# Where the mean is subtracted in three normalisations, and when the gates of the experts are computed

## What the program computes

```
def layer_norm(x, g, b):
    mu = jnp.mean(xf, axis=-1, keepdims=True)
    var = jnp.mean(jnp.square(xf - mu), axis=-1, keepdims=True)
    return ((xf - mu) * lax.rsqrt(var + LN_EPS) * g + b)

def moe_ffn(h, router, w1, w3, w2):
    logits = h @ router
    top_val, top_idx = lax.top_k(logits, TOP_K)
    top_w = jax.nn.softmax(top_val, axis=-1)
    gate = jnp.sum(one_hot(top_idx, N_EXPERTS) * top_w[..., None], axis=-2)
    # sum over e of gate[..., e] * swiglu(h, w1[e], w3[e], w2[e])
```

## Time and profile before

| | |
|---|---|
| median of 3 runs | 2023.13 us (2023.11 to 2023.94) |
| profiled execution | 2023.13 us, span 2021.2 us |
| mean granted PE clock | 0.985 of full speed |
| busy: PE, PEld, DVE, ACT, POOL | 96%, 81%, 67%, 53%, 4% of the span |
| DMA | 456.89 MB, mean 226 GB/s |

### The profile page before, as it was taken

One profiled execution on the slowest core, in us unless ns is written; L12 is line 12 of the kernel. 1 busy time (PEld: TensorE's weight loads), 2 busy tenths in 40 slices (PEclk: granted clock), 3 DMA queues, 4 the chain that ended last, 5 costly groups with the idle time before them and its releaser, 6 DMA issues. The chain is left out here.

```text
span 2021.2 us, 25922 instructions
## 1 busy us (share of the span) xinstructions
PE 1945.7 (96%) x10571; PEld 1637.4 (81%) x10571; DVE 1351.8 (67%) x1547; ACT 1063.4 (53%) x1206; POOL 82.3 (4%) x152
## 2 busy tenths in 40 slices
PE   6999999899989999998999999999999999999995
PEld 5677889899976778888888788888888888888884
DVE  3744237644335643265687988979889798897986
ACT  2233233444332323244676776767767677676773
POOL 4002000100020011001000000000000000000000
PEclk9999999999999999998899999999999999999998
DMA  7223225355433232153499999999999999899992
GB/s 206 84 72 108 63 73 189 125 167 167 145 80 104 77 103 85 42 167 116 170 372 328 346 363 313 373 328 346 368 307 374 335 342 369 305 375 337 334 374 107
DMA packets 260479, 456.89 MB, mean 226 GB/s; under 512 B 32218, under 2 KB 111274, under 8 KB 260356
## 3 DMA queue, kind: packets, MB, share of 16 engines
q1 hardware_dynamic: 258966, 454.74, 65.5%
q10 hardware_dynamic: 1390, 0.44, 0.1%
HBM read 452.11 MB, written 3.04 MB: 225 GB/s over the span
## 5 line engine op out<-in xcount | busy, mean ns | idle before, releaser
L380 DVE TENSOR_TENSOR wl<-ring,wh 128x2048 fp32r<-128x2048 f32 x385 | 880.7, 2289 | 252.0 <-ACT wh L374 248.7
L374 ACT ACTIVATE wh<-ring 128x2048 fp32r<-128x2048 f32 x385 | 737.1, 1917 | 322.6 <-PE ps L349 322.6
L349 PE MATMUL ps<-hT,ring 128*128 128x288 f32 (+1 forms) x1376 | 360.6, 414 | 7.9 <-ACT hT L660 5.3
L349 PE MATMUL ps<-wh,xgh 128*128 128x512 f32 x896 | 355.5, 397 | 2.3 <-DVE wl L380 2.3
L349 PE MATMUL ps<-wl,xgh 128*128 128x512 f32 x896 | 350.2, 391 | 0.0
L349 PE MATMUL ps<-wh,xgl 128*128 128x512 f32 x896 | 350.2, 391 | 0.0
L349 PEld LDWEIGHTS ps<-hT,ring 128*128 128x128 f32 (+1 forms) x1376 | 253.5, 190 | 82.4 <-issue 12.3
L349 PEld LDWEIGHTS ps<-wh,xgh 128*128 128x128 f32 x896 | 168.8, 188 | 40.4 <-DVE wl L380 5.7
L349 PEld LDWEIGHTS ps<-wh,xgl 128*128 128x128 f32 x896 | 168.7, 188 | 36.1
L349 PEld LDWEIGHTS ps<-wl,xgh 128*128 128x128 f32 x896 | 169.0, 189 | 33.5
L349 PE MATMUL ps<-wh,gEh 128*128 128x512 f32 x448 | 143.4, 401 | 0.0
(11 more groups left out here) (405 smaller groups left out, 2398.1 us busy)
## 6 DMA issues: line engine op xcount, KB each, us to landing
ring<-in_moe_w SPq DMA_DIRECT2D x336, 1024.0 KB, 5.5
ring<-in_w_in SPq DMA_DIRECT2D x38, 1024.0 KB, 5.2
ring<-in_ffn_w SPq DMA_DIRECT2D x33, 1024.0 KB, 5.2
ring<-in_w_out SPq DMA_DIRECT2D x8, 1024.0 KB, 5.4
ring<-in_w_in SPq DMA_DIRECT2D x32, 128.0 KB, 3.0
ring<-in_w_oa SPq DMA_DIRECT2D x16, 256.0 KB, 3.8
ring<-in_w_ob SPq DMA_DIRECT2D x8, 512.0 KB, 4.9
resid<-in_x_prompt SPq DMA_DIRECT2D x1, 1024.0 KB, 5.4
```

What stands on the lines that cost most here:

```text
L349: ins = nc.tensor.matmul(*a, **k)
L374: nc.scalar.activation(wh[:, k % WS, :], ring[:, s:s + SLOT], ACT.Copy).then_inc(hi_ready, 1)
L380: ins = nc.vector.tensor_tensor(wl[:, k % WS, :], ring[:, s:s + SLOT], wh[:, k % WS, :].bitcast(F32), ALU.subtract)
```

## The change

The split of the eight subtractions is turned round, and the gates are computed earlier. In `centred`, POOL subtracts the mean from tiles 4 to 7, four in place of five. In `normalised`, DVE subtracts it from tiles 0 to 3, and does so between the variance and the wait for the root, ahead of the reciprocal; the three subtractions between the products are gone, and the products of tiles 4 to 7 wait for POOL. One constant, XC_DVE = 4, replaces XC_POOL = 5 and also HL_DVE = 4, so the split of the low halves stays as it is. In the expert stage the wait for `rt_exp` and the six operations of the gates move from behind `low_half(1)` to the place between the copy of the indices and the marks (five of the six ahead of `selm` and `sel_ready`, the last one behind it).

```diff
-        XC_POOL = 5
+        XC_DVE = 4
...
             pool.wait_ge(nst_ready, 2 * q + 2)
-            for k in range(XC_POOL):
+            for k in range(XC_DVE, KD):
                 nc.gpsimd.tensor_tensor(hT[:, k, :], hT[:, k, :], mean, ALU.subtract).then_inc(xc_ready, 1)
...
+            dve.wait_ge(nst_ready, 2 * q + 2)
+            for k in range(XC_DVE):
+                c(nc.vector.tensor_tensor(hT[:, k, :], hT[:, k, :], mean, ALU.subtract))
             dve.wait_ge(nstd_ready, q + 1)
             c.link(nc.vector.reciprocal(rsd, sdev))
             for k in range(KD):
-                if k < XC_POOL:
-                    dve.wait_ge(xc_ready, XC_POOL * q + k + 1)
-                else:
-                    c.link(nc.vector.tensor_tensor(hT[:, k, :], hT[:, k, :], mean, ALU.subtract))
+                if k >= XC_DVE:
+                    dve.wait_ge(xc_ready, (KD - XC_DVE) * q + k - XC_DVE + 1)
                 nc.vector.tensor_tensor(tn[:, k, :], hT[:, k, :], rsd, ALU.mult).then_inc(tn_ready, 1)
...
                     c.link(V.tensor_copy(rtop[:, :, 2:4], ridx[:, :, 0:2].bitcast(U32)))
+                    dve.wait_ge(rt_exp, 1)
+                    c.link(V.tensor_scalar(rw[:, :, 2:3], rw[:, :, 1:2], 1.0, None, ALU.add))
+                    c.link(V.reciprocal(rw[:, :, 2:3], rw[:, :, 2:3]))
+                    c.link(V.tensor_tensor(rw[:, :, 3:4], rw[:, :, 2:3], rw[:, :, 1:2], ALU.mult))
...
                     c.sync()
+                    c(V.tensor_tensor(gate, rsel[:, :, 0:NE], each(rw[:, :, 2:3]), ALU.mult))
+                    c(V.tensor_tensor(gate2, rsel[:, :, NE:2 * NE], each(rw[:, :, 3:4]), ALU.mult))
                     ins = V.tensor_tensor(selm, rsel[:, :, 0:NE], rsel[:, :, NE:2 * NE], ALU.add)
                     ins.then_inc(sel_ready, 1)
+                    c.sync()
+                    c(V.tensor_tensor(gate, gate, gate2, ALU.add))
...
                     low_half(1)
-                    dve.wait_ge(rt_exp, 1)
-                    c.link(V.tensor_scalar(rw[:, :, 2:3], rw[:, :, 1:2], 1.0, None, ALU.add))
-                    c.link(V.reciprocal(rw[:, :, 2:3], rw[:, :, 2:3]))
-                    c.link(V.tensor_tensor(rw[:, :, 3:4], rw[:, :, 2:3], rw[:, :, 1:2], ALU.mult))
-                    c(V.tensor_tensor(gate, rsel[:, :, 0:NE], each(rw[:, :, 2:3]), ALU.mult))
-                    c.link(V.tensor_tensor(gate2, rsel[:, :, NE:2 * NE], each(rw[:, :, 3:4]), ALU.mult))
-                    c.link(V.tensor_tensor(gate, gate, gate2, ALU.add))
                     keep(c, "dve")
```

More of the change, by code:

```diff
@@ L2051, in program @@
                                                        sem("gT_ready"))
-        HL_DVE = 4
         hf_ready, hl_dve, hl_pool = sem("hf_ready"), sem("hl_dve"), sem("hl_pool")
@@ L2065, in _ @@
                     centred(pool, 0)
-                    for k in range(HL_DVE, KD):
+                    for k in range(XC_DVE, KD):
                         pool.wait_ge(h_ready, k + 1)
@@ L2086, in _ @@
                                 if u == 0 and c == 0:
-                                    if k < HL_DVE:
+                                    if k < XC_DVE:
                                         pe.wait_ge(hl_dve, k + 1)
                                     else:
-                                        pe.wait_ge(hl_pool, k - HL_DVE + 1)
+                                        pe.wait_ge(hl_pool, k - XC_DVE + 1)
                                 ins = rel.mm(ps[2 * u + c][:, 0:T], w0[u][0][:, k, P * c:P * c + P], hTl[:, k, :],
@@ L2165, in _ @@
                                                 ALU.mult, ALU.add).then_inc(hf_ready, 1)
-                    for k in range(HL_DVE):
+                    for k in range(XC_DVE):
                         dve.wait_ge(h_ready, k + 1)
@@ L2434, in _ @@
                     centred(pool, 2)
-                    pool.wait_ge(xc_ready, 3 * XC_POOL)
+                    pool.wait_ge(xc_ready, 3 * (KD - XC_DVE))
                     for j, h in enumerate((htokh, htokl)):
```

## The result

The changed kernel takes 2036.12 us (median of 4 runs, 2034.21 to 2036.70) against 2023.12 us (4 runs, 2021.30 to 2023.94) for the kernel before: 13.0 us more, ratio 1.0063, 95% interval [1.0046, 1.0082]. It is slower, as forecast; the forecast was 2034.4. The profiled execution spans 2034.3 us against 2021.2, so its trace holds the 13.1 us to be explained.

What follows compares the result with a forecast made beforehand. PE was taken to set the pace, waiting only for each norm's first tile, so lateness there is lost at the end. 2023.13 us, +8.9 for the norms and +2.4 for the routing, gave 2034.4, range 2029 to 2038.5.

Steps and rivals of the forecast that it cites:

- The norms' term: Norms: DVE's subtractions ahead of the reciprocal make each first tile 3.02 us late; three norms, less 0.2, give +8.9 us.
- turns of 0.97: Norms: DVE and POOL operations with two SBUF inputs take turns, a pair costing about 0.97 us.
- the bounds 0.6 and 4.0: First tile of each norm: 0.6 us late without hindrance between DVE and POOL, 4.0 if pairs cost both whole operations.
- Rival (a): Norms: DVE and POOL don't hinder each other in this order; +3.6 us, 2026.7, chance 0.07.
- rival (b): Norms: no overlap, each pair costs 1.24 us, 4.0 per norm; +14 us, 2037 to 2039, chance 0.07.
- Rival (c): Norms: the last tile decides, not the first; about -2 us with the routing, chance 0.02.
- half the hindrance: Norms: DVE and POOL hinder each other half as much, 1.8 us per norm; +7.4, 2030.5, chance 0.08.
- The stall of 0.2 us: Dense stage: PE's stall of 0.17 us for DVE's low halves (L2169) goes away, -0.2 us.
- The routing's term: Routing: DVE's wait for the exponential delays the marks and PE's counts; +2.4 us, from 2.0 to 3.7.
- the lower bound: Routing: L2583 starts when DVE's low half ends, at 968.2 in place of 966.24, +2.0 us.
- The clock: PE's clock: shifts in when it rises or falls are likely, either sign, giving +-2 us around the forecast.
- Rival (d): Last two norms' slow-clock stretches: all at 2.4 GHz would save 16.2 us, giving 2018, faster; chance 0.02.

Runs made afterwards that it cites:

- after_warm: Changed kernel plus unused matmuls on PE, 32 at each norm's wait and 8 ahead of each of two routing waits: 2026.52 us, ratio 1.0010 to the kernel before.
- after_no_pool: Changed kernel with POOL's subtractions given to DVE, tiles 4 to 7 each ahead of its product: 2029.29 us, ratio 1.0030 to the kernel before.
- norms_only: Changed kernel with the gates back at their old place, so only the norms differ from the kernel before: 2031.64 us, ratio 1.0045 to it.
- routing_only: Kernel before with only the gates moved, norms as before: 2026.01 us, ratio 1.0017 to the kernel before.
- before_warm: Kernel before plus unused matmuls on PE, 20 at each norm's wait and 8 at the wait for pos_ready: 2013.91 us, ratio 0.9963.
- warm_pool3: Kernel before plus the unused matmuls of before_warm, with POOL subtracting three tiles in place of five: 2012.66 us, ratio 0.9943.

## Why the prediction was right

**The bound.** PE waited for the first tile of each norm, three times, and what the first tile lost was lost at the end: no later stretch of the changed kernel gave back any of it. This holds at the clock that these kernels have behind a norm. At the full clock PE is fast enough to want the later tiles as well, and then 1.4 of the 3.0 us came back at norm 1 (after_warm).

**The norms' term.** +3.02 for each first tile, measured +3.0, three times. The steps were met: turns of 0.97 (x4 in 3.97), a first product of 0.46 without POOL, PE's wait 8.25 where 8.3 was said. The choice between the bounds 0.6 and 4.0 rested on rows of before that already held the two engines' operations side by side, and after_no_pool shows both the 0.6 and its cause. Rival (a), no hindrance, and rival (b), whole operations in a row, fall: a pair costs 0.97 and not 1.24. The Trainium skill's page "SBUF — State Buffer", "Who interferes with whom", is right that such operations hinder each other, but the blocking for a whole instruction that it states overstates the price here. Rival (c), the last tile, falls for this kernel: in the first norm the last product came 0.9 late (1.0 was forecast) and ACT's last tile 2.0, and PE waited for neither. Of the sums, half the hindrance should read +7.6 and not +7.4 with the +2.4 of the routing; nothing hangs on it.

**The low halves.** The stall of 0.2 us went, 0.3 in fact: the 32 products with low halves took 4.32 us in place of 4.60. That POOL's own low halves would be done in time was taken for granted and nearly failed (last section).

**The routing's term.** +2.4 taken from 2.0 to 3.7, measured +2.6. The wait of DVE was forecast at 3 us (3.20), PE's late start at 2.0 (2.1), and the extra over 2.0 is the half-rate of the last short matmuls, as was said. Only the lower bound rested on the wrong engine: DVE's low half was to end last, and the trace has DVE wait 0.70 for PE's counts.

**The clock.** This is the part that the sum put at nothing, with +-2 around it: 13.0 against 11.3. The trace has +1.5 behind norm 0 and +2.1 between norms 1 and 2, -1.4 ahead of the first norm, which has nothing to do with the change, and -0.5 from the experts' first product on. Two things speak for the moments as they fell and against a regular price of longer waits. norms_only has the same norms and the same waits, and lost 3.1 and 3.3 us in the two middle stretches, not 4.2 and 5.1; behind norm 0 its clock was low for 6.8 us and not 10.2. And the fall near 637 us, some 40 behind the start of norm 1, stands at nearly the same place in routing_only (629.67), whose norms are those of before:

```profile
629.67:633.08 3.41, 3.41 (x11) 2.37 (x12) 1.84 (x5) 1.09 (x2) 0.00 (x0) 0.50 0.00 0
```

The two parts run alone summed to 11.4. So the chains account for 11.3 of the 13.0 us. How far the measured time lies from them, and on which side, is as far as these runs show a matter of the moments, and the close hit of 2034.4 is in part luck. With one trace for each kernel, and the kernel before itself between 2021 and 2028, a small regular part isn't excluded.

**Rival (d)**, the clock as a gain, did not come from the change. Of the 16.2 us that it put on the slow stretches before_warm took 9.3 by other means, nearly all of it behind norm 2.

## What to carry to other kernels

Ahead of moving work to an idle moment of one engine, look for rows in which the same kinds of operations already ran on both engines together: the price of an operation is its length there, not its length alone. Work that fills a short gap is only free if it is shorter than the gap: here 0.6 us between variance and reciprocal was filled with 1.6 us of work, 4.0 with POOL beside it, on the one chain that PE waited for. And where PE must wait some microseconds for such a chain, a few matmuls with no use in that wait can be worth more than a rearrangement of the chain, but only where PE finds work ready at the faster pace: 8.0 us behind norm 2, 1.0 behind norm 1, nothing behind norm 0.

## What the hardware showed that was not expected

The two engines do not always take turns. In the dense stage of the kernel before, POOL's last three low halves took 2.68 us beside DVE's. In the changed kernel, DVE ran its four low halves at their free pace and the weight split behind them, while a single operation of POOL, recorded as started 0.13 us ahead of DVE's first, lasted from 380.15 to 384.71:

```profile
379.49 2.68 POOL L2069 TENSOR_TENSOR hTl<-hT,hTh 128x288 fp32r<-128x288 f32 x3
```

```profile
380.15 4.56 POOL L2069 TENSOR_TENSOR hTl<-hT,hTh 128x288 fp32r<-128x288 f32 x1
```

```profile
380.28 1.55 DVE L2169 TENSOR_TENSOR hTl<-hT,hTh 128x288 fp32r<-128x288 f32 x4
...
381.76 2.28 DVE L380 TENSOR_TENSOR wl<-ring,wh 128x2048 fp32r<-128x2048 f32 x1
```

Five operations of DVE were done within one of POOL. It was no single case: in after_warm POOL's longest low half took 4.53 us. In the changed kernel PE came to these tiles just after; in after_warm, where PE is faster, it waited 1.0 us for them. What decides whether the engines alternate or one is passed over was not tried.

The granted clock also fell where no norm is near, at 51.50 in the kernel before and at 636.74 and 892.74 in the changed one. What PE did just ahead of each, as busy time by stretch, first before, then changed:

```profile
48.09:51.50 3.41, 2.15 (x21) 1.68 (x20) 1.25 (x8) 1.08 (x2) 0.00 (x0) 1.00 0.41 130
```

```profile
633.33:636.74 3.41, 2.15 (x20) 1.70 (x21) 1.70 (x9) 1.08 (x2) 0.00 (x0) 1.00 0.29 90
889.33:892.74 3.41, 1.87 (x15) 1.30 (x13) 1.98 (x6) 0.63 (x2) 0.00 (x0) 1.00 0.55 164
```

PE was not idle there but busy with gaps, 1.87 to 2.15 us of 3.41, the longest gap 1.26, 1.26 and 1.54 us. The same code of the other kernel kept the clock. The fall near 51 us stands in six of the nine traces (not in the changed kernel, routing_only and warm_pool3), whatever was edited. Each costs about a microsecond (1.4 near 51 us), and single runs of one kernel differ by several: of the 42 runs of the kernel before, those above 2026 us have a mean granted clock of 0.982 to 0.984, those below 2022.2 of 0.984 or 0.985.
